# One step of a hybrid decoder on one core: the first weight group is loaded in smaller pieces, and one page scaling changes places with a weight split

## The reference, cut to what matters

```python
def even_project(x, w_in, pos):
    h = x @ w_in                       # (264, 2048) @ (2048, ...): groups 0 to 9 of the kernel
    q, kvc, kvs, kvw, gates, glu = jnp.split(h, EVEN_SPLITS, axis=-1)

def compress(rows, pe, w):             # rows: the 2048 past tokens of each of 8 samples, by pages of 128
    blk = rows[:, :nb * CMP_BLOCK].reshape(B, nb, CMP_BLOCK, KV_HEADS, HEAD_DIM)
    summ = jnp.mean((blk * pe[None, None, :, None, :]).astype(jnp.float32), axis=2)
    return jnp.einsum('bngd,de->bnge', summ, w)
```

## Time and profile before

| | us |
|---|---|
| median of 3 runs | 2439.32 (2438.43 to 2439.43) |
| the profiled execution, same clock as the runs | 2438.98 |
| its span, first to last instruction | 2437.1 |
| TensorE busy | 2388.9 (98%) |
| VectorE busy | 1474.5 (61%) |
| ScalarE busy | 1071.9 (44%) |
| DMA, whole span | 516.80 MB, mean 212 GB/s |

### The profile page before, as it was taken

The page is one execution under the profiler, slowest core; times in us unless marked ns, Lnnn a source line. Parts: engine busy times, 40 slices in busy tenths (PEclk is TensorE's granted clock), DMA queues, the critical chain, the costliest instruction groups (busy, mean ns, idle before and its releaser), DMA issues.

```text
span 2437.1 us, 50797 instructions
## 1 busy us (share of the span) xinstructions
PE 2388.9 (98%) x20548; PEld 2258.7 (93%) x20548; DVE 1474.5 (61%) x1732; ACT 1071.9 (44%) x1302; POOL 94.1 (4%) x180
## 2 busy tenths in 40 slices
PE   8999998999999999999999999999999999999997
PEld 6888862779999999999999999999999999999996
DVE  6777778675866444444444778768754444444456
ACT  3333321454575353354353445446743534433433
POOL 0000014220000000000000010000000000000000
PEclk9999999999999999999999999999999999999998
DMA  9999669895555555555555564454555544454451
GB/s 377 352 327 325 213 202 319 303 332 224 186 188 214 199 213 200 211 202 183 205 178 184 174 227 172 169 175 173 173 188 174 186 176 181 180 181 181 179 184 70
DMA packets 102974, 516.80 MB, mean 212 GB/s; under 512 B 13088, under 2 KB 29536, under 8 KB 56640
## 3 DMA queue, kind: packets, MB, share of 16 engines
q1 hardware_dynamic: 91872, 467.90, 53.8%
q0 software_dynamic: 10976, 47.13, 5.6%
HBM read 508.59 MB, written 18.95 MB: 216 GB/s over the span
## 4 chain that ended last, share of the span: by engine, by line
PE 91%; DVE 4%; ACT 1%; issue 1%; DMA 1%; POOLq 0%; POOL 0%; SPq 0%; ACTq 0%; DVEq 0%
PE psa L441 28%; PE psa L442 27%; PE psa L443 27%; PE psm L477 2%; PE psa L645 1%; ACT whi L1100 1%; PE psm L841 1%; PE psa L820 1%; DVE page L1625 1%; DVE wlo L1609 1%; DVE stage L1835 1%; PE psa L638 1%; PE psm L672 1%; DMA page<-in_cmp 0%; PE psm L829 0%
## 5 line engine op out<-in xcount | busy, mean ns | idle before, releaser
L1609 DVE TENSOR_TENSOR wlo<-wraw,whi 128x2048 fp32r<-128x2048 f32 x356 | 815.7, 2291 | 770.3 <-ACT whi L1100 770.0
L1100 ACT ACTIVATE whi<-wraw 128x2048 fp32r<-128x2048 f32 x356 | 682.1, 1916 | 968.1 <-PE psa L443 962.1
L441 PE MATMUL psa<-xhi,whi 128*128 128x264 f32 (+1 forms) x2096 | 605.3, 289 | 13.7 <-DVE wlo L1609 12.0
L442 PE MATMUL psa<-xlo,whi 128*128 128x264 f32 (+1 forms) x2096 | 600.4, 286 | 0.0
L443 PE MATMUL psa<-xhi,wlo 128*128 128x264 f32 (+1 forms) x2096 | 599.0, 286 | 0.0
L443 PE MATMUL psa<-hhi,wlo 128*128 128x264 f32 x2048 | 581.4, 284 | 0.0
L442 PE MATMUL psa<-hlo,whi 128*128 128x264 f32 x2048 | 581.3, 284 | 0.0
L441 PE MATMUL psa<-hhi,whi 128*128 128x264 f32 x2048 | 580.8, 284 | 0.0
L443 PE MATMUL psa<-nhi,wlo 128*128 128x264 f32 x1536 | 435.2, 283 | 0.0
L442 PE MATMUL psa<-nlo,whi 128*128 128x264 f32 x1536 | 434.9, 283 | 0.0
L441 PE MATMUL psa<-nhi,whi 128*128 128x264 f32 x1536 | 434.9, 283 | 0.0
(11 more groups left out here) (424 smaller groups left out, 1565.2 us busy)
## 6 DMA issues: line engine op xcount, KB each, us to landing
wraw<-in_w SPq DMA_DIRECT2D x356, 1024.0 KB, 4.8
page<-in_cmp SPq DMA_DIRECT2D x128, 384.0 KB, 5.2
kbuf<-in_selk SPq DMA_DIRECT2D x64, 192.0 KB, 4.0
kbuf<-in_selk POOLq DMA_DIRECT2D x64, 192.0 KB, 4.2
vbuf<-in_selv SPq DMA_DIRECT2D x64, 192.0 KB, 4.2
vbuf<-in_selv POOLq DMA_DIRECT2D x64, 192.0 KB, 4.3
o_win<-in_win POOLq DMA_DIRECT2D x8, 1533.0 KB, 7.6
kbuf<-in_wink SPq DMA_DIRECT2D x8, 768.0 KB, 5.4
```

Source lines behind the costliest of these rows:

```text
L441: mm(out, wh, hi[:, k, 0:w], start=(k == 0), stop=False)
L442: mm(out, wh, lo[:, k, 0:w], start=False, stop=False)
L1100: A(whi[:, p % 2, :], wraw[:, p, :], ACT.Copy).then_inc(s.hi_ready, 1)
L1609: V.tensor_tensor(wlo[:, p % 2, :], wraw[:, p, :], whi[:, p % 2, :].bitcast(F32), ALU.subtract).then_inc(s.lo_ready, 1)
```

## The change

It has two parts. First, quarter 0 of group 0 comes in three pieces, of one, one and two k tiles (`EARLY`), both for x and for w, each split by itself, and TensorE takes each as it becomes ready: first the high-by-high products, then the two others. Quarter 1 too starts with its high-by-high products. For this, group 0 has its own function, `first_group`, in place of the call of `group`; quarters 2 and 3 run in the order of before. The first wait of POOL is now for the third weight quarter (`raw2`). Second, in the loop over groups 2 to 7, VectorE scales pair 1 ahead of the split of quarter 1.

```diff
+        EARLY = ((0, 1), (1, 1), (2, 2))
+        x_early = [s.v0, s.v1, s.x_in]
+        w_early = [s.v2, s.v3, s.raw0]
@@ SP
+            for i, (k, m) in enumerate(EARLY):
+                sp.dma_start(x[:, k:k + m, :]..., io.x[:, k * NT:(k + m) * NT]).then_inc(x_early[i], 16)
+                sp.dma_start(wraw[:, 0, 512 * k:512 * (k + m)], io.w[0:1, 0, :, 512 * k:512 * (k + m)]...).then_inc(w_early[i], 16)
-            for p in range(4):
+            for p in range(1, 4):
                 sp.dma_start(x[:, 4 * p:4 * p + 4, :]..., io.x[:, 4 * p * NT:(4 * p + 4) * NT])...
                 weights(0, p)
@@ POOL
             pool.dma_start(ptab[:], io.ptab).then_inc(s.ptab_in, 16)
-            pool.wait_ge(s.raw0, 16)
+            pool.wait_ge(s.raw2, 16)
             pool.dma_start(const[:], io.const).then_inc(s.const_in, 16)
@@ TensorE
-            group(0, xhi, xlo, (s.x_ready, 0), first_hooks)
+                for i, (k, m) in enumerate(EARLY):
+                    if i < 2:
+                        pe.wait_ge(s.x_hi, 2 * i + 2)
+                    else:
+                        pe.wait_ge(s.x_hi, 5)
+                        pe.wait_ge(s.hi_ready, 1)
+                    for kk in range(k, k + m):
+                        for n in range(4):
+                            term(whi, xhi, 0, n, kk, kk == 0, False)
+                    pe.wait_ge(s.x_ready, k + m)
+                    if i == 2:
+                        pe.wait_ge(s.lo_ready, 1)
+                    for kk in range(k, k + m):
+                        for n in range(4):
+                            term(whi, xlo, 0, n, kk, False, False)
+                            last = term(wlo, xhi, 0, n, kk, False, False)
+                last.then_inc(s.piece_done, 1)
+                pe.wait_ge(s.x_hi, 6)
+                pe.wait_ge(s.hi_ready, 2)
++                for kk in range(4):
+                    for n in range(4):
+                        term(whi, xhi, 1, n, kk, False, False)
+                pe.wait_ge(s.x_ready, 8)
+                pe.wait_ge(s.lo_ready, 2)
++                for n in range(4):
+                    for kk in range(4):
+                        term(whi, xlo, 1, n, kk, False, False)
+                        last = term(wlo, xhi, 1, n, kk, False, False)
+                last.then_inc(s.piece_done, 1)
+                for p in range(2, 4):
+                    pe.wait_ge(s.lo_ready, p + 1)
+                    pe.wait_ge(s.x_ready, 4 * p + 4)
...
+                        first_hooks(p, n)
@@ ScalarE
+            for i, (k, m) in enumerate(EARLY):
+                act.wait_ge(x_early[i], 16)
+                A(xhi[:, k:k + m, 0:NT], x[:, k:k + m, :], ACT.Copy).then_inc(s.x_hi, 1)
+                act.wait_ge(w_early[i], 16)
+                A(whi[:, 0, 512 * k:512 * (k + m)], wraw[:, 0, 512 * k:512 * (k + m)], ACT.Copy)\
+                    .then_inc(s.x_hi if i < 2 else s.hi_ready, 1)
@@ VectorE
+            for i, (k, m) in enumerate(EARLY):
+                dve.wait_ge(s.x_hi, 2 * i + 1)
+                ins = V.tensor_tensor(xlo[:, k:k + m, 0:NT], x[:, k:k + m, :], xhi[:, k:k + m, 0:NT]..., ALU.subtract)
...
+                V.tensor_tensor(wlo[:, 0, 512 * k:512 * (k + m)], wraw[...], whi[...], ALU.subtract)...
@@ VectorE, loop over groups 2 to 7
                 page_scale(j, 0)
+                page_scale(j, 1)
                 split(j, 1)
-                page_scale(j, 1)
                 tok_copy(j, 0)
```

More of the change, by code:

```diff
@@ L288, in pages @@
                         .then_inc(pg[r % 4], 16)
-            for p in range(4):
+            for i, (k, m) in enumerate(EARLY):
+                sp.dma_start(x[:, k:k + m, :].rearrange("p k t -> p (k t)"), io.x[:, k * NT:(k + m) * NT]).then_inc(x_early[i], 16)
+                sp.dma_start(wraw[:, 0, 512 * k:512 * (k + m)], io.w[0:1, 0, :, 512 * k:512 * (k + m)].rearrange("a q n -> q (a n)"))\
+                    .then_inc(w_early[i], 16)
+            for p in range(1, 4):
                 sp.dma_start(x[:, 4 * p:4 * p + 4, :].rearrange("p k t -> p (k t)"), io.x[:, 4 * p * NT:(4 * p + 4) * NT])\
-                    .then_inc((s.x_in, s.x1_in, s.x2_in, s.x3_in)[p], 16)
+                    .then_inc((s.x1_in, s.x2_in, s.x3_in)[p - 1], 16)
                 weights(0, p)
@@ L495, in first_hooks, with first_group, term @@
                     reduce_pair(0, 2 * p - 4 + n // 2)
-            group(0, xhi, xlo, (s.x_ready, 0), first_hooks)
+            def first_group():
+                def term(w, v, p, n, kk, start, stop):
+                    return mm(psa[:, n, 0:NT], w[:, p % 2, 512 * kk + 128 * n:512 * kk + 128 * n + 128], v[:, 4 * p + kk, 0:NT],
+                              start=start, stop=stop)
+                for i, (k, m) in enumerate(EARLY):
[22 more added lines that the diff above has]
+                pe.wait_ge(s.lo_ready, 2)
+                for n in range(4):
+                    for kk in range(4):
+                        term(whi, xlo, 1, n, kk, False, False)
[4 more added lines that the diff above has]
+                    pe.wait_ge(s.x_ready, 4 * p + 4)
+                    for n in range(4):
+                        for kk in range(4):
+                            term(whi, xhi, p, n, kk, False, False)
+                            term(whi, xlo, p, n, kk, False, False)
+                            last = term(wlo, xhi, p, n, kk, False, p == 3 and kk == 3)
+                        if p == 3:
+                            last.then_inc(s.bank_done, 1)
+                        elif n == 3:
+                            last.then_inc(s.piece_done, 1)
+                        first_hooks(p, n)
@@ L498, in _ @@
+            first_group()
             SECOND = ((1, 1), (2, 1), (2, 3), (3, 3))
@@ L650, in values @@
             def values(u):
-                pe.wait_ge(vin[u % 5], landed(u))
+                pe.wait_ge(vin[u % 5], landed(u) + (16 if u % 5 < 4 else 0))
                 if u >= 8:
@@ L1113, in later @@
                 split(G, 3)
-            for q in range(4):
-                act.wait_ge((s.x_in, s.x1_in, s.x2_in, s.x3_in)[q], 16)
+            for i, (k, m) in enumerate(EARLY):
[4 more added lines that the diff above has]
+                    .then_inc(s.x_hi if i < 2 else s.hi_ready, 1)
+            for q in range(1, 4):
+                act.wait_ge((s.x1_in, s.x2_in, s.x3_in)[q - 1], 16)
                 A(xhi[:, 4 * q:4 * q + 4, 0:NT], x[:, 4 * q:4 * q + 4, :], ACT.Copy).then_inc(s.x_hi, 1)
-                if q < 2:
+                if q == 1:
                     split(0, q)
@@ L1633, in _ @@
             V.memset(st[:], 0.0).then_inc(s.hid_ready, 1)
-            for q in range(4):
-                dve.wait_ge(s.x_hi, q + 1)
+            for i, (k, m) in enumerate(EARLY):
+                dve.wait_ge(s.x_hi, 2 * i + 1)
+                ins = V.tensor_tensor(xlo[:, k:k + m, 0:NT], x[:, k:k + m, :], xhi[:, k:k + m, 0:NT].bitcast(F32), ALU.subtract)
+                if i < 2:
+                    step(ins)
+                    dve.wait_ge(s.x_hi, 2 * i + 2)
+                else:
+                    ins.then_inc(s.x_ready, m)
+                    dve.wait_ge(s.hi_ready, 1)
+                V.tensor_tensor(wlo[:, 0, 512 * k:512 * (k + m)], wraw[:, 0, 512 * k:512 * (k + m)],
+                                whi[:, 0, 512 * k:512 * (k + m)].bitcast(F32), ALU.subtract).then_inc(s.x_ready if i < 2 else s.lo_ready, 1)
+            for q in range(1, 4):
+                dve.wait_ge(s.x_hi, 5 + q)
                 V.tensor_tensor(xlo[:, 4 * q:4 * q + 4, 0:NT], x[:, 4 * q:4 * q + 4, :], xhi[:, 4 * q:4 * q + 4, 0:NT].bitcast(F32),
                                 ALU.subtract).then_inc(s.x_ready, 4)
-                if q < 2:
+                if q == 1:
                     split(0, q)
```

## The result

The changed kernel is slower, by a little: median 2442.15 us (2437.57 to 2445.62, 22 runs) against 2438.48 for the kernel before (2434.87 to 2441.5, 22 runs). The ratio is 1.0015, 95% interval 1.001 to 1.0021, so +3.7 us (2.4 to 5.1). The forecast was 2437.1, range 2433.8 to 2440.0. The profiled execution took 2441.18, its span is 2439.3.

The account below looks back on a forecast made before the run. TensorE, busy 98% of the span, was taken to bound the kernel, with the DMA stream full until 42 us. From 2438.98, minus 0.3 (part 1) and 1.94 (part 2), gives 2436.7; the median's 0.34 makes about 2437.1, range 2433.8 to 2440.0.

Parts of the forecast that it names:

- First matmul at 5.2, first quarter through by 13.6: Start of group 0: smaller first pieces let TensorE begin 6.3 us earlier, at 5.2, and end the first quarter at 13.6.
- the stream does not starve for them: Loads at the start: four more DMA issues on SP cost 1.8 us there, without emptying the DMA stream behind them.
- 0.4 later (if the DMA stream decides, and the short rows slow it ...): Page pair 7's transfer: latest bound on its landing, against 0.9 us earlier at best; 0.3 earlier was taken.
- Constants 11.2 us behind their release: Constant transfers, released by the third weight quarter at 14.9: same distance as before, so landing at 26.1, bounds 20 and 35.
- Quarter 4 starts 6.4 us behind the constants, harmless until 26.5, slower from 29.5: Group 0, first reduction to quarter 4: constants cost nothing until 26.5; from 29.5 the whole change is slower than before.
- rival 3: Wait before the first reduction, third quarter: constants come too late; at 35, with slow matmuls, 2447 us; chance 0.08.
- Rival 1, the clock: TensorE's new gaps of 2.2 and 3.2 us: clock falls in the second, quarter 4 near 35.2, 2438.6 us; chance 0.22.
- The meetings with the DMA stream take the head start: Page pairs 1 and 7 come by DMA: of 6.3 us, 0.9 are left at quarter 4 and 0.3 after pair 7.
- Part 2: -1.94: Groups 2 to 7: scaling pair 1 ahead of the split cuts first reductions from 1.84 (group 2: 1.74) to 1.50 us.

Follow-up runs that it names:

- e5: Changed kernel with the first quarter of x and of w loaded by one DMA each, compute still in pieces; 2437.42 us, ratio 0.9997 to the kernel before.
- e4: Kernel before, with only the constants released by the third weight quarter instead of the first; 2438.76 us, ratio 1.0005.
- e12: Changed kernel with whole first-quarter DMAs, piecewise compute and 27 unused matmuls before the first page reduction; one run, 2439.11 us.
- e7: Changed kernel with 40 unused matmuls in TensorE's idle stretch before the first page reduction; 2438.56 us, ratio 1.0001 to the kernel before.
- e3: Changed kernel with the old order in the loop, page pair 1 scaled behind the split; 2441.07 us, ratio 1.0014 to the kernel before.
- e13: e5 with constants released by the first weight quarter's last piece and 12 unused matmuls ahead of quarter 3; 2435.37 us, ratio 0.9988 to the kernel before.
- e2: Kernel before with only page pair 1 scaled ahead of the split in groups 2 to 7; 2435.7 us against 2438.22, ratio 0.999.
- e17: Kernel before with the first quarter of w loaded in three pieces, x still in one DMA; one run, 2438.98 us.
- e18: Kernel before with three pieces each of x and w, each read from its own contiguous array; one run, 2442.05 us.
- e16: Kernel before with the first quarter of x loaded in three pieces, w still in one DMA; one run, 2442.11 us.
- e11: Kernel before with the first quarter loaded by six DMAs cut by partitions (0-31, 32-63, 64-127), rows kept full; 2440.77 us, ratio 1.001.
- e1: Changed kernel with the constants released by the last piece of the first weight quarter instead of the third quarter; 2438.44 us, ratio 1.0006 to the kernel before.
- e6: Kernel before with only the first quarter's DMAs cut into three pieces each for x and w; 2442.07 us, ratio 1.0017.

## Why the prediction was wrong, point by point

- *First matmul at 5.2, first quarter through by 13.6*: right, 5.63 and 14.2. The change does what it says.
- *"the stream does not starve for them"*, and *"0.4 later (if the DMA stream decides, and the short rows slow it ...)"*: **the step that failed.** The transfers were counted as free because the old ones overlap at a share of 1.02: the third weight quarter's landing, 14.9, was worked out without a term for them, and page pair 7 was given 0.4 at most. The new ones move 268 GB/s, and the quarter lands at 17.06. With whole transfers (e5) it is 14.78. The term was put at nothing there and is 2.3, and the first reduction is late by as much (31.35 against 29.02 in e5).
- *Constants 11.2 us behind their release*: this was counted from the landing of the weight quarter (7.21 to 18.4). Counted so it is 12.3 (17.06 to 29.35), 1.1 more. From POOL's own row it is 12.0 (17.36 to 29.35), against 10.9 before (7.50 to 18.4), 11.3 in e4 and 12.0 in e5; why it grew isn't shown.
- *Quarter 4 starts 6.4 us behind the constants, harmless until 26.5, slower from 29.5*: the rule of rival 3, and it held. It was 6.7 in e4 and e12 at full clock; the 0.3 is in the 24 matmuls, which take 3.15 us up to the next reduction and not 2.9. In the changed kernel it was 8.6, with 1.9 for the clock. The constants at 29.35 stand almost on its threshold, and the clock did the rest. Rival 3 had a chance of 0.08, though the prediction's own bounds for the constants were 20 and 35.
- *Rival 1, the clock*: came together with rival 3, not apart from it. Priced at 2.3 to 2.7 us of quarter 4, measured 1.87 in the changed kernel (against e7 and the kernel before), 1.5 in e5 (against e12) and 2.7 in e3. But for the far end of rival 3, the two rivals were kept apart, though one makes the gap in which the other happens.
- *The meetings with the DMA stream take the head start*: right. e12 and e13 show it with everything else repaired: 33.51 for Q4, and 50.24 for pair 7.
- *Part 2: -1.94*: right, 1.50 instead of 1.84 in group 3. From pair (1, 7) to the last reduction of group 7, the changed kernel and e2 both regain 1.9 us, and e3 nothing. By time e2 measured -2.5 (-4.6 to -0.5).

The sum of Q4, by the experiments: 33.71, nothing for the piecewise start itself (33.51 in e12), +1.7 from e12 to e5 (35.22; 1.5 of it the clock behind the idle stretch), +2.7 for the small transfers (37.93; 2.3 of it the later reduction). Minus 1.94 in the loop this leaves 2.3 at the span, which grew by 2.2. That the two agree so closely is partly luck, since marks of one kernel differ by up to 1.4 us between executions. The medians say 3.7 (2.4 to 5.1); what the 1.4 between are, if anything, isn't shown.

The Trainium skill's page "DMA: Bandwidth & Descriptors" (Rules for kernel authors) says to coalesce small transfers. I set it aside because transfers overlapped, and the measurement decides for the page's direction: six transfers in place of two cost 2.3 us. The fixed cost of about 2 us that the page gives for one transfer issued from GpSimd, paid four times one after another, would have made 8 (an estimate from the page's figure), and no run here shows that.

## What to carry to other kernels

Find the resource that the next meeting point waits for before giving an engine a head start; here the DMA stream was full for 42 us, and 6 us of earlier matmuls could only wait. Cutting a transfer in front of a full stream delays everything behind it, so look at the rate in that window and not at the first landing. When a load moves behind others, compute its landing with an error bar and compare it with the time at which its cover ends; and a wait of some us in front of TensorE is to be priced together with the lower clock behind it.

## What the runs showed of the hardware that was not expected

- Three pieces of 256 to 512 KB for w in place of one of 1 MB cut the rate from 418 to 280 GB/s over 5 us (e17), whether the source was strided or contiguous (277, e18, with x cut too). Cutting x alone left 377 (e16).
- Loads to 32 or 64 partitions with full rows: 222 GB/s at a DMA share of 1.03 (e11), about half of the 418 with all 128. The busy share does not show that a stream is slow.
- The clock: behind 1.85 us of idle TensorE, at 23.65, it was at the upper of its two levels (2.4 GHz; 24 matmuls started within 2.9 us), behind 4.50 us at the lower one (1.2 GHz; 0.53 granted over 6 us), as behind 4.01 us in e5 and 4.53 in e1. The Trainium skill's page "TensorE: Matmul & The Clock Gate" (Why this matters for your kernels) warns of gaps between bursts; the trace agrees.
- ScalarE's table load waits with its first activation: further waits in front of that moved it from 0.85 to 7.89 us (e6).
